# Encoder with product-key experts: last output chunks by tile, other visit counts beside gate stores, V's first weights inside u's last rows, negated maximum, last norm by tile

## The reference

```
h = rmsnorm(x);  proj = h @ w_in                       # 1024 -> 3584
na  = neighbourhood_attention(q, k, v, rpb)             # 8 heads of 64, softmax
ret = bidirectional_retention(q, k, v, gate, decays)    # 4 heads of 128
x = x + concat(na, ret) @ w_out
h = rmsnorm(x);  q = h @ w_q                           # 8 heads x 2 x 128
s = q . sub_keys;  top 16 of each half; top 16 of the 256 sums -> experts e, gates g (softmax)
x = x + sum over the 8*16 chosen experts:  g * gelu(h . u[e]) * v[e]
y = rmsnorm(x)                                         # x * rsqrt(mean(x*x)+eps) * final_g
```

## Time and profile before

| | us |
|---|---|
| median of 3 runs | 2512.49 (2505.99 to 2517.33) |
| the profiled execution | 2510.96 |
| its span | 2509.2 |
| mean granted PE clock | 0.975 of full speed |

### The profile page before, as it was taken

The page is one execution under the profiler, slowest core; times in us unless marked ns, Lnnn a source line. Parts: engine busy times, 40 slices in busy tenths (PEclk is TensorE's granted clock), DMA queues, the critical chain, the costliest instruction groups (busy, mean ns, idle before and its releaser), DMA issues.

```text
span 2509.2 us, 34594 instructions
## 1 busy us (share of the span) xinstructions
PE 2384.2 (95%) x12777; PEld 2031.1 (81%) x12777; DVE 1851.9 (74%) x3571; ACT 927.3 (37%) x1426; POOL 1333.3 (53%) x892
## 2 busy tenths in 40 slices
PE   7988999999999997999999999899899999999997
PEld 7868999999867766887788788778688778888886
DVE  4673796454367796669999697587597688888886
ACT  4443454654334323232233233232233333333333
POOL 0000698000342444648777676588584388888860
PEclk9987999999999998999999999999999999999999
DMA  5443677877754555746567578968978899999994
GB/s 166 154 133 122 208 223 222 258 219 229 240 181 132 172 165 196 249 155 204 183 200 218 176 248 273 332 211 261 358 254 264 313 329 348 342 349 348 345 369 162
DMA packets 252679, 596.84 MB, mean 238 GB/s; under 512 B 35792, under 2 KB 118224, under 8 KB 251872
## 3 DMA queue, kind: packets, MB, share of 16 engines
q1 hardware_dynamic: 182496, 385.69, 46.4%
q0 software_dynamic: 67712, 201.61, 24.4%
q10 hardware_dynamic: 2304, 7.34, 1.0%
HBM read 521.12 MB, written 73.40 MB: 237 GB/s over the span
## 4 chain that ended last, share of the span: by engine, by line
PE 34%; POOL 8%; DMA 4%; DVE 3%; issue 3%; ACT 1%; SPq 1%; DVEq 0%; ACTq 0%
PE ps L811 31%; POOL a_got L479 4%; POOL picked L474 3%; DMA raw<-in_experts 3%; PE ps L1057 2%; POOL sp_lo L470 1%; DMA picked<-in_experts,vidx 1%; DVE acc L1540 1%; SPq L359 1%; ACT v_hi L715 0%; ACT sp_hi L697 0%; DVE acc_odd L1540 0%; DVE w_lo L1572 0%; DVE v_lo L1580 0%; DVE sp_lo L1589 0%
## 5 line engine op out<-in xcount | busy, mean ns | idle before, releaser
L474 POOL DMA_INDIRECT picked<-in_experts,vidx x384 | 501.3, 1305 | 632.9 <-PE ps L811 219.8
L811 PE MATMUL ps<-ht_hi,sp_hi 128*128 128x256 f32 (+1 forms) x2048 | 706.5, 345 | 26.7 <-POOL sp_lo L470 14.1
L811 PE MATMUL ps<-ht_lo,sp_hi 128*128 128x256 f32 (+1 forms) x2048 | 694.7, 339 | 0.0
L811 PE MATMUL ps<-ht_hi,sp_lo 128*128 128x256 f32 (+1 forms) x2048 | 693.6, 339 | 0.0
L479 POOL DMA_INDIRECT a_got<-acts,aidx x384 | 526.5, 1371 | 123.5 <-issue 109.0
L470 POOL TENSOR_TENSOR sp_lo<-raw,sp_hi 128x1024 fp32r<-128x1024 f32 x112 | 302.1, 2711 | 357.8 <-ACT sp_hi L697 357.4
L811 PEld LDWEIGHTS ps<-ht_hi,sp_hi 128*128 128x128 f32 x2048 | 392.8, 192 | 73.1 <-POOL sp_lo L470 19.2
L811 PEld LDWEIGHTS ps<-ht_hi,sp_lo 128*128 128x128 f32 x2048 | 392.2, 191 | 42.0
L811 PEld LDWEIGHTS ps<-ht_lo,sp_hi 128*128 128x128 f32 x2048 | 392.8, 192 | 37.0
L1589 DVE TENSOR_TENSOR sp_lo<-raw,sp_hi 128x1024 fp32r<-128x1024 f32 x144 | 176.3, 1224 | 232.2 <-ACT sp_hi L697 228.9
L705 ACT ACTIVATE act_g<-ps 128x256 f32<-128x256 f32 (+1 forms) x256 | 125.8, 491 | 555.5 <-PE ps L811 514.7
(11 more groups left out here) (187 smaller groups left out, 3585.2 us busy)
## 6 DMA issues: line engine op xcount, KB each, us to landing
raw<-in_experts SPq DMA_DIRECT2D x256, 512.0 KB, 4.1
v_raw<-in_experts SPq DMA_DIRECT2D x128, 512.0 KB
raw<-in_front SPq DMA_DIRECT2D x104, 512.0 KB
acts<-act_g SPq DMA_DIRECT2D x128, 256.0 KB
act_in<-acts SPq DMA_DIRECT2D x128, 192.0 KB
acts<-act_g SPq DMA_DIRECT2D x128, 128.0 KB
gates<-stage SPq DMA_DIRECT2D x16, 1024.0 KB
g_in<-gates SPq DMA_DIRECT2D x128, 128.0 KB
```

The costliest lines, as they stand in the source:

```text
L474: pool.indirect_dma_start(picked[n % SLOTS][:, :], None, v_rows, bass.IndirectOffsetOnAxis(ap=vidx[:, n // P, n % P:n % P + 1], axis=0)).t ...
L811: last = pe.matmul(out, l, r, start=start and k == 0, stop=stop and k == 2, skip_group_check=True)
```

## The change

- The last two output chunks are done tile by tile (`v_last_pair`): both chunks for tile 0, then both for tile 1, and so on. The split of chunk `C_WQ+2` moves behind: on ACT behind `turned_hi` of tile 1, on DVE behind `norm`.
- `MID_AT`: entries 12 and 28 become 13 and 29, so POOL's fetches of these two groups lie one step later.
- Visit weights: 4 in a store step, 12 elsewhere. By the formula: 5 visits in each group of store steps (12 before), 32, 35 and 35 in the gate windows (30, 32, 32), and 15 in steps 249 to 255 (11). Eight steps within or at the edge of the gate windows and step 255 have three visits; before, none had more than two.
- SP loads the weights of v rows 0 and 1 behind step 250 and not behind step 255; the weight tiles get separate places, and row 0's can be made before u's last matmul.
- `reduce_max` writes the negated maximum itself; the reciprocal moves ahead of the next score.
- The last norm is done per tile: squares of tiles 0 and 1 at v rows 20 and 24, means at 25 and 29, roots at 28 and 32, scaling at 33 and 37; the others one by one at the end.

```
-MID_AT = {2: 2, 5: 3, 8: 3, 12: 4, 20: 4, 23: 2, 28: 4, 34: 4, 37: 2, 42: 3, 47: 3, 51: 2}
+MID_AT = {2: 2, 5: 3, 8: 3, 13: 4, 20: 4, 23: 2, 29: 4, 34: 4, 37: 2, 42: 3, 47: 3, 51: 2}
...
@@ sync
-            for t in DENSE[:-1]:
-                sp.wait_ge(S[f"gate_out{t}"], 16 * PARTS)
-            for k in range(2):
-                sp.wait_ge(act_out[k], 8 * (STEPS - 28))
-            for r in range(2):
-                load_weights(r)
+                if step == STEPS - 6:
+                    for t in DENSE[:-1]:
+                        sp.wait_ge(S[f"gate_out{t}"], 16 * PARTS)
+                    for k in range(2):
+                        sp.wait_ge(act_out[k], 8 * (STEPS - 28))
+                    for r in range(2):
+                        load_weights(r)
@@ scalar
-                for c in range(C_OUT + 1, C_WQ):
+                for c in range(C_OUT + 1, C_WQ - 1):
                     hi(q, c + AHEAD)
...
+                    if i == 1:
+                        hi(q, C_WQ - 1 + AHEAD)
...
+                if step == STEPS - 1:
+                    v_part(1)
+                    weights_hi(0)
                 gelu(step)
...
+                if r in (20, 24):
+                    last_square(r // 4 - 5)
+                if r in (28, 32):
+                    last_root(r // 4 - 7)
+            for t in range(2, NT):
+                last_square(t)
+                last_root(t)
@@ tensor
+            def v_last_pair(q, c0):
+                pe.wait_ge(*counted(q, "lo_ready", c0 + 2))
+                for i in range(TILES[q]):
+                    for c in range(c0, c0 + 2):
+                        sl = slot_of(q, c)
+                        for kk in range(2):
+                            k, cols = 2 * (c % 4) + kk, slice(kk * 512, kk * 512 + 512)
+                            last = exact(ps[:, 2 + i, :], (ht_hi[q][:, k, tile_cols(i)], ht_lo[q][:, k, tile_cols(i)]),
+                                         (sp_hi[:, sl, cols], sp_lo[:, sl, cols]), k == 0, k == KD - 1)
+                        if c == c0 + 1:
+                            last.then_inc(S["v_done"], 1)
+                        elif i == TILES[q] - 1:
+                            last.then_inc(S["v_used"], 1)
...
-                for c in range(C_OUT + 2, C_WQ):
+                for c in range(C_OUT + 2, C_WQ - 2):
...
+                v_last_pair(q, C_WQ - 2)
@@ vector
-                        steps.add(dve.reduce_max(s["mx"][:, u:u + 1], scored, AX.X))
-                        steps.settle()
-                        dve.tensor_scalar(s["nmx"][:, u:u + 1], s["mx"][:, u:u + 1], -1.0, None, ALU.mult
-                                          ).then_inc(S["na_max"], 1)
+                        dve.reduce_max(s["nmx"][:, u:u + 1], scored, AX.X, negate=True).then_inc(S["na_max"], 1)
...
-                        lo(q, c + AHEAD)
+                        if c < C_WQ - 1:
+                            lo(q, c + AHEAD)
                         visits(2 * q)
...
                 norm(q, 1, s["g2"])
+                lo(q, C_WQ - 1 + AHEAD)
...
                 if r == 0:
+                    dve.wait_ge(S["hot_ready"], 32 * SPARSE)
+                    dve.wait_ge(S["gate_evac"], 32 * SPARSE)
+                if r == 1:
                     dve.wait_ge(S["a_done"], STEPS)
-                    dve.wait_ge(S["gate_evac"], 32 * SPARSE)
...
-            weight = [11 if gate_window(step + 1) else 8 for step in range(first_free, STEPS)]
+            def stores(step):
+                return any(0 <= step - GATES_AT[t] - GATE_ROWS < PARTS for t in DENSE[:-1])
+            weight = [4 if stores(step) else 12 for step in range(first_free, STEPS)]
...
+                if r in (25, 29):
+                    mean_square((r - 25) // 4)
...
+                if r in (33, 37):
+                    scaled((r - 33) // 4)
...
-            final(0)
+            mean_square(2)
+            scaled(2)
             for d in range(SPARSE):
                 dve.wait_ge(S["y_tile"], d + 1)
                 dve.tensor_tensor(x2d[:, d, :], ps[:, 2 + 2 * d:4 + 2 * d, :].rearrange("p c n -> p (c n)"),
                                   x2d[:, d, :], ALU.add).then_inc(S["y_added"], 1)
-            final(1)
+                if d:
+                    mean_square(SPARSE + d - 1)
+            for d in range(SPARSE):
+                if d == SPARSE - 1:
+                    mean_square(NT - 1)
+                scaled(SPARSE + d)
```

More of the change, by code:

```diff
@@ L1233, in front, with inverse @@
                     visits(q * ((c > 3) + (c > 7)))
+                def inverse(m):
+                    dve.wait_ge(*counted(q, "na_exp", m + 1))
+                    u = NA_HEADS * FIRST_TILE[q] + m
+                    steps.add(dve.reciprocal(s["prec"][:, u:u + 1], s["psum_"][:, u:u + 1]))
                 add_mask(q, 0)
@@ L1256, in front @@
                         u = NA_HEADS * FIRST_TILE[q] + n - 3
-                        dve.wait_ge(*counted(q, "na_exp", n - 2))
-                        steps.add(dve.reciprocal(s["prec"][:, u:u + 1], s["psum_"][:, u:u + 1]))
+                        if units <= n <= units + 1:
+                            inverse(n - 2)
                         steps.settle()
@@ L1571, in weights_lo @@
                 dve.wait_ge(S["w_hi_ready"], r + 1)
-                dve.tensor_tensor(w_lo[:, r % 2], w_f[:, r % 2], w_hi[:, r % 2].bitcast(F32), ALU.subtract
+                dve.tensor_tensor(w_lo[r % 2][:, :], w_f[r % 2][:, :], w_hi[r % 2][:, :].bitcast(F32), ALU.subtract
                                   ).then_inc(S["w_lo_ready"], 1)
@@ L1683, in _, with mean_square, scaled @@
             visits(2 * P - done)
+            def mean_square(t):
+                col = slice(2 * NT + t, 2 * NT + t + 1)
+                dve.wait_ge(S["end_ss"], t + 1)
+                dve.tensor_scalar(s["ms"][:, col], s["ssq"][:, col], 1.0 / D_MODEL, EPS, ALU.mult, ALU.add
+                                  ).then_inc(S["end_ms"], 1)
+            def scaled(t):
+                col = slice(2 * NT + t, 2 * NT + t + 1)
+                dve.wait_ge(S["end_rms"], t + 1)
+                steps.add(dve.reciprocal(s["rstd"][:, col], s["rms"][:, col]))
+                steps.settle()
+                o = acc[t][:, :] if t < SPARSE else x2d[:, t - SPARSE, :]
+                dve.scalar_tensor_tensor(o, o, s["rstd"][:, col], fgain[:, :], ALU.mult, ALU.mult
+                                         ).then_inc(S["y_out"], 1)
             v_part(0)
```

71 lines of the change are left out of this document (30 added, 41 removed).

## The result

The changed kernel is slower, by a little: the medians are 2518.46 us after and 2510.97 us before, 20 runs each, and the ratio is 1.0032 with a 95% interval of 1.0017 to 1.0048. The forecast was 2477. The profiled execution took 2515.49 us, its span is 2513.7, against 2510.96 and 2509.2 before: 4.5 us more in the traces, 7.5 in the runs. The mean granted clock is 0.976 (0.975 before).

The account below looks back on a forecast made before the run. PE, busy 95% of the span, was taken as the bound. Terms 17 + 5 + 0 + 4.2 + 5 + 0.5 + 0 + 2.4 = 34 us off 2510.96 gave 2477 us, with an 8-in-10 range of 2460 to 2500.

Parts of the forecast that it names:

- The visits' new place: Gate windows and last steps: 14 moved visits make DVE late about three steps each time; 0 net (-6.8 to +20 us).
- The store term: Store steps behind two gate windows: fewer visits relieve full DMA, saving 17 us of PE idle and 5 of lost clock.
- The first (stores alone): Rival, store steps: stores alone fill the queue, so 22 us of stores and clock become 9; 2490 us, chance 0.16.
- the third: Rival: DVE late in all three gate windows, two more windows costing 10 us each; 2497 us, chance 0.12.
- fourth: Rival, gate windows: self-sustaining DVE lateness passed on whole to PE, 70 us more; 2547 us, chance 0.07.
- The second rival: Second gate window runs clean, lost clock returns whole, v's start gives all; 2462 us, inside the forecast's 0.62.
- Output chunks by tile: Output projections of q=1 and q=0: norm turns come earlier, q=1's wait 2.1 and not 5.03; gain 5 us (1 to 9).
- V's first weights: Start of v: earlier loads cut PE's 5.20 us wait by 2.5, plus 1.7 of clock; 4.2 us (0 to 8.6).
- it may cost up to 2: Start of v: row 2's load still waits for the last u step; a cost of up to 2 us.
- Last norm by tile: Kernel's end: last scaling 3.7 us earlier, less 1.3 for new DVE work in v; net 2.4 us (0 to 4).
- Negated maximum: Attention stages: 48 operations of 154 ns go, mostly covered by projection work on PE; gain 0.5 us (0 to 2).
- `MID_AT`: Fetches at 13 and 29 move one u step past POOL's splits; 0 us, give or take one gap of 3.

Follow-up runs that it names:

- h_small_visits: Changed kernel with DVE's part of each tile 1 visit from number 125 on cut to 128 of 1024 columns, fetches kept whole; ratio to before 0.9846.
- g_early_new: Changed kernel, new visit weights, with tile 1's last 112 single-activation fetches issued early, beside visits 8 to 82 of the q=1 front; ratio to before 1.0079.
- c_no_store_visits: Kernel before without the 24 visits beside the gate stores and without their fetches, nothing moved; ratio to before 0.9924.
- a_old_weights: Changed kernel with the old visit weights (11 and 8) put back, all other edits kept; ratio to before 0.9982.
- e: Changed kernel without the eight third visits of its gate windows, rows neither fetched nor added; ratio to before 0.9904.
- b: Kernel before with only the new visit weights (4 and 12); ratio to before 1.0065.
- d: Kernel before with each gate store cut to one of its sixteen rows (64 KB for 1 MB), all visits kept; ratio to before 0.9891.
- j: Changed kernel with old visit weights and 56 single-activation fetches issued early, two beside each of front visits 4 to 31; ratio to before 0.9912.
- n: Kernel before, none of the change's edits, with 56 single-activation fetches issued early beside front visits; ratio to before 0.9989.

## Why the prediction was wrong

**The step that failed** is "The visits' new place", which took 0 net for eight steps with three visits and so kept 17 us beside the stores and 5 of clock. Forecast for steps 198 to 255 was -22; it was +16.8. That is 39 of the 42 us by which the median misses the forecast. It failed in two ways:

- I priced a dry visit where it occurs, and let DVE be "late for about three steps and then in step again". It isn't: with DVE never idle POOL's issue takes 3.65 us, which makes the next visit late. The third window went from 115 to 123 us, with seven dry visits (13.8 us) where there had been none. Without DVE's part of the visits (h_small_visits), and without POOL's second issue (g_early_new), it is clean at the same visit counts.
- I counted the store steps' traffic by DVE's visits. It goes by POOL's fetches, and POOL entered these steps with empty slots: 12 fetches for 9 visits in the first piece. And of the 7 visits taken out of each group only 4 and 5 left the piece around it, since its edge steps got a third one. So the 17 us never came.

**The store term itself** was sound in its cause and too large. With DVE kept in step (h_small_visits) the store pieces gain 13 of the 17 + 5. DMA is still at 1.02 there. c_no_store_visits, without these visits, gets 16.

**The rivals.** The first (stores alone) fits the time beside the stores, but c_no_store_visits shows that its cause is not there. What happened is the third and fourth, DVE late in all windows, at a size between them, and with the store gain lost besides, which neither had. The second rival's clean window is what h_small_visits shows (125 to 113). I took the first gate window, in step by the earlier trace rows, as what a window does. Before the change the first and the third were in step, but a_old_weights, with the same visit counts, has the third late, so this window was near the edge already.

**Output chunks by tile** (5 forecast): the turns came as said, 2.08 for 5.03 in q=1, and 2.07 for 2.95 in q=0. But two more waits follow the first, 1.06 and 2.36 where it was 0.18 and 3.43, and the one ahead of the second half grew from 1.94 to 2.41. From PE's stop ahead of the output projection's second half to its restart at 1002.09 (1010.01) it is 48.5 us before and 46.9 after, so q=1 gives 1.6 and both 2.5.

**V's first weights** (4.2 forecast): the hop from 5.20 to 2.89 is as worked out, but "it may cost up to 2" was 3.87. Row 2's load still starts when u ends, and ACT waits 7.52 us for it. In a_old_weights, where DVE is free in time, row 0 does not wait and row 2 waits 4.43:

```profile
1955.01 0.47 PE L831 MATMUL ps<-v_hi,w_hi 128*128 128x512 f32 x1 [0.21 <-issue]
1963.81 0.77 PE L831 MATMUL ps<-v_hi,w_hi 128*128 128x512 f32 x1 [4.43 <-DVE w_lo L1615]
```

So most of the wait moved two rows on: both together are 6.8 us in the changed kernel and 4.6 in a_old_weights, against 5.2. The term is under 1 us, or a loss of 1.6.

**Last norm by tile** (2.4 forecast): the tail went from 13.9 to 9.1 us, 4.8 where 3.7 was said. In v the four such kernels a, e, h and the changed one drift back 2.3 to 4.3 us from row 4 to row 127, against the kernel before, and b, c and d, without the edit, 0.8 to 2.4. Net about 3.

**Negated maximum** and `MID_AT` are below what the fronts vary by. Together the other edits were forecast at 12. Tail and turns give 6 to 7, the profiled fronts at step 128 average 10.0 ahead with them (four kernels) and 4.5 without (b, c, d and the kernel before), and j against n measures 19 (12 to 27). The sum was right or low, and that is partly luck, as the terms of the output chunks and of v's first weights were too large. Where in the front the rest comes from stays open.

## What to carry to other kernels

When work is moved off a crowded stretch, count what the slowest engine in its chain still does there, not what its consumer does: a fetcher that is behind brings its traffic along. A stretch that runs without gaps beside an engine that is 95% busy can be near to a late one: here visits of 1.3 us more made it late, and in a_old_weights it was late with none more. So take slack from the engine that is late, or take instructions off the one behind it, before moving work in. And a free place for an issue is judged by the waits of what is queued behind it, as the turn of q=1 showed.

## What the runs showed of the hardware

- An indirect fetch that POOL issues while DVE runs operations with two tensor inputs back to back ends 0.82 us (median) behind the end of such a run; an operation with one tensor input behind the run (`hot_a`) doesn't hold it. Alone it takes 0.95, for a row as for a single value. The same instruction so takes 0.95 or 3.65 us by what DVE does. With DVE's visits cut to an eighth the mean fell from 1.69 to 1.08 for rows.
- Nine and twelve row fetches more, with their visits, beside 8 MB of stores in 512-byte pieces lengthened PE's 56 and 58 us by 7 and 9. Without them DMA stood at 0.90 and PE's clock at 1.00.
- The kernel before has a late window (125.6 us) and two in step (114.2) in the same execution. Its runs range from 2490 to 2520 us; whether late windows make that spread is not shown, as one run is profiled.
